# A small expert block put last in a block on one Trainium2 core: its rows reach the sum by a selection, and the stored rows are read back ahead of the next weights

## What is computed

```python
def expert_block(args):
    xb, e = args
    return swiglu(xb, lp['w_eg'][e], lp['w_eu'][e], lp['w_ed'][e])
yb = lax.map(expert_block, (xin, block_e)).reshape(n_rows, d)
return jax.ops.segment_sum(yb[dest] * sw[:, None], st, num_segments=t)
# then: layer_norm(alpha * x + gate * y), rms_norm, x + 0.5 * swiglu(h, w1, w3, w2)
```

## Time and profile before

| what | value |
|---|---|
| three runs, us | 2492.45, 2494.76, 2496.57 (median 2494.76) |
| the profiled execution, us | 2494.52 |
| its span, us | 2493.2 |
| granted PE clock, mean | 0.992 |
| PE busy | 2417.6 us, 97% |
| DVE, ACT, POOL busy | 57%, 42%, 12% |

### The profile page before, as it was taken

The page is one execution under the profiler, slowest core; times in us unless marked ns, Lnnn a source line. Parts: engine busy times, 40 slices in busy tenths (PEclk is TensorE's granted clock), DMA queues, the critical chain, the costliest instruction groups (busy, mean ns, idle before and its releaser), DMA issues.

```text
span 2493.2 us, 30650 instructions
## 1 busy us (share of the span) xinstructions
PE 2417.6 (97%) x12306; PEld 1875.2 (75%) x12306; DVE 1415.3 (57%) x2052; ACT 1040.7 (42%) x1570; POOL 288.8 (12%) x249
## 2 busy tenths in 40 slices
PE   6999999999999989999999899999999999999999
PEld 4877868687777767777666688888888777888887
DVE  3675776768636766555555574344444767543442
ACT  2424434343536346655555462223333555422221
POOL 0010112112132301111111000000122000000000
PEclk9999999999999989999999999999999999999999
DMA  7324243332446378999999822332332111323222
GB/s 277 114 72 168 86 142 126 118 126 75 151 161 224 105 268 348 424 423 424 422 422 423 327 78 91 95 110 86 92 117 77 34 47 64 110 78 108 94 80 80
DMA packets 116227, 428.10 MB, mean 172 GB/s; under 512 B 16040, under 2 KB 30632, under 8 KB 90352
## 3 DMA queue, kind: packets, MB, share of 16 engines
q1 hardware_dynamic: 91488, 377.42, 41.0%
q10 hardware_dynamic: 13440, 25.17, 2.8%
q0 software_dynamic: 11152, 23.49, 2.7%
HBM read 411.60 MB, written 31.72 MB: 178 GB/s over the span
## 4 chain that ended last, share of the span: by engine, by line
PE 75%; DMA 13%; DVE 7%; ACT 4%; issue 1%; SPq 0%; ACTq 0%; POOLq 0%; DVEq 0%
PE bank L754 19%; PE bank L756 18%; PE bank L755 18%; DMA pair<-in_ed 9%; PE bank L1329 2%; DVE HLB L426 1%; PE bank L1310 1%; PE bank L1312 1%; PE bank L1311 1%; PE bank L1367 1%; ACT HLB L415 1%; PE bank L1672 1%; DMA raw<-in_wxbc 1%; DMA raw<-in_wz 1%; PE bank L1695 1%
## 5 line engine op out<-in xcount | busy, mean ns | idle before, releaser
L426 DVE TENSOR_TENSOR HLB<-raw,HLB 128x1024 fp32r<-128x1024 f32 (+1 forms) x286 | 345.6, 1211 | 373.6 <-ACT HLB L415 373.3
L754 PE MATMUL bank<-HTh,HLB 128*128 128x512 f32 (+1 forms) x1358 | 545.2, 401 | 9.9 <-DVE HLB L426 7.5
L756 PE MATMUL bank<-HTh,HLB 128*128 128x512 f32 (+1 forms) x1358 | 528.7, 389 | 0.0
L755 PE MATMUL bank<-HTl,HLB 128*128 128x512 f32 (+1 forms) x1358 | 525.5, 387 | 0.0
L415 ACT ACTIVATE HLB<-raw 128x1024 fp32r<-128x1024 f32 (+1 forms) x294 | 289.5, 991 | 298.6 <-PE bank L756 270.8
L754 PEld LDWEIGHTS bank<-HTh,HLB 128*128 128x128 f32 x1358 | 256.8, 189 | 90.3 <-issue 27.5
L756 PEld LDWEIGHTS bank<-HTh,HLB 128*128 128x128 f32 x1358 | 257.1, 189 | 57.1
L755 PEld LDWEIGHTS bank<-HTl,HLB 128*128 128x128 f32 x1358 | 257.2, 189 | 52.8 <-issue 1.9
L755 PE MATMUL bank<-FAl,HLB 128*128 128x512 f32 x352 | 138.9, 395 | 0.0
L756 PE MATMUL bank<-FAh,HLB 128*128 128x512 f32 x352 | 138.9, 395 | 0.0
L754 PE MATMUL bank<-FAh,HLB 128*128 128x512 f32 x352 | 138.9, 395 | 0.0
(11 more groups left out here) (618 smaller groups left out, 4435.3 us busy)
## 6 DMA issues: line engine op xcount, KB each, us to landing
raw<-in_f SPq DMA_DIRECT2D x120, 512.0 KB, 3.4
ht_pair<-in_eu SPq DMA_DIRECT2D x32, 1024.0 KB, 24.8
pair<-in_ed SPq DMA_DIRECT2D x32, 1024.0 KB, 25.4
raw<-in_wada SPq DMA_DIRECT2D x40, 512.0 KB, 4.0
raw<-in_eg SPq DMA_DIRECT2D x17, 1024.0 KB, 19.8
pair<-in_eu SPq DMA_DIRECT2D x17, 1024.0 KB, 19.6
tmp_pair<-in_eg SPq DMA_DIRECT2D x16, 1024.0 KB, 24.5
ht_pair<-in_eg SPq DMA_DIRECT2D x16, 1024.0 KB, 25.2
```

Source lines behind the costliest of these rows:

```text
L426: self.nc.vector.tensor_tensor(lo, raw, hi.bitcast(F32), ALU.subtract).then_inc(*self.w_lo.next(n))
L754: mm(bank, ah, bh, start=(start and i == 0), stop=False)
L755: mm(bank, ah, bl, start=False, stop=False)
L756: ins = mm(bank, al, bh, start=False, stop=(stop and i == n - 1))
```

## The change

- The order of the blocks becomes 0 to 29, then 31, then 30 (`place_of`), so that a small block is the last, and two whole blocks, 29 and 31, come one behind the other. Positions are still counted 0 to 31.
- On PE and ACT, down of position 30 goes ahead of gate and up of position 31 (the argument `straight`), so no block's work separates it from its own middle. The tiles are loaded in that order, and the last 12 go to places by a new list.
- The kept rows are those of the small block: one eviction and one remainder in place of two each, `YOh` and `YOl` of 128x512, half the columns below partition 64 and half from it on; `tok31` comes from `ixs` by one more instruction. The zeros of `no_rows` cover half rows.
- The four reads of `y_scratch` are issued ahead of the first four tiles of the dense layer, into the parts of `YI` in the order 0, 2, 3, 1 (`back`), each with its own wait.
- The splits of those four tiles move, on ACT from ahead of the combination to behind `act_logs` and between the gains, on DVE from the start of the combination to between its remainders.
- `kept(0, 0)` issues two matmuls without use (`keep_busy`) before it waits for the kept rows.

```diff
-    def __init__(self, nc, small, source, slots, turns, halves, loads, hi_made, lo_made, pe_out):
+    def __init__(self, nc, small, straight, source, slots, turns, halves, loads, hi_made, lo_made, pe_out):
...
-            self.at.append(turns[0][n] if n < len(turns[0]) else turns[1][(n - len(turns[0])) % len(turns[1])])
+            late = n - 6 * len(small) + len(turns[2])
+            self.at.append(turns[0][n] if n < len(turns[0]) else turns[2][late] if late >= 0
+                           else turns[1][(n - len(turns[0])) % len(turns[1])])
...
+        down = [("ed", 0), ("ed", 1)]
         for j in range(n + 1):
+            if j == straight:
+                self.add(j - 1, "down", down)
...
-            if j:
-                self.add(j - 1, "down", [("ed", 0), ("ed", 1)])
+            if j and j != straight:
+                self.add(j - 1, "down", down)
...
-        YOh, YOl = (here("YO" + p, [128, 8, 128], FR) for p in "hl")
+        YOh, YOl = (here("YO" + p, [128, 4, 128], FR) for p in "hl")
...
             for j in range(len(blocks)):
+                if j == S.kept:
+                    down(j - 1)
                 (small_gate_up if tiles.small[j] else gate_up)(j)
...
-                if j:
+                if j and j != S.kept:
                     (small_down if tiles.small[j - 1] else down)(j - 1)
                 turn_mid(j)
-            down(len(blocks) - 1)
+            (small_down if S.kept else down)(len(blocks) - 1)
...
+        def back(i):
+            return YI[:, (0, 2, 3, 1)[i], :, :]
...
                 bank = psum.take(pe, ("yl", t, b))
+                if t == b == 0:
+                    keep_busy(bank, 2)
...
                     k = 2 * b + j
-                    pe.wait_ge(*dve_out.when(("yo", 31, k // 4)))
-                    mm(bank[:, half(j)], YOh[:, k, :], PICK[:, half(t)], start=(j == 0), stop=False)
-                    mm(bank[:, half(j)], YOl[:, k, :], PICK[:, half(t)], start=False, stop=False)
+                    p = slice(64 * (k // 4), 64 * (k // 4) + 64)
+                    pe.wait_ge(*dve_out.when(("yo", 31, 1)))
+                    mm(bank[:, half(j)], YOh[p, k % 4, :], PICK[p, half(t)], start=(j == 0), stop=False)
+                    mm(bank[:, half(j)], YOl[p, k % 4, :], PICK[p, half(t)], start=False, stop=False)
...
+                if j == S.kept:
+                    act.wait_ge(*dve_out.when("wrows"))
+                    activation(YOh[:, :, :], psum[("yo", j, 1)][:, :].rearrange("p (k n) -> p k n", k=4), ACT.Copy,
+                               scale=WROWS[:, KEPT:KEPT + 1]).then_inc(*act_out.next(("yo", j, 1)))
+                    return
...
-                if j == S.kept:
-                    for n in range(2):
-                        activation(YOh[:, 4 * n:4 * n + 4, :], psum[("yo", j, n)][:, :].rearrange("p (k n) -> p k n", k=4),
-                                   ACT.Copy, scale=weight).then_inc(*act_out.next(("yo", j, n)))
-                    return
...
+                if j == S.kept:
+                    last(j - 1)
...
-                if j:
+                if j and j != S.kept:
                     last(j - 1)
...
         def act_combine():
-            ring.hi(act, "f13", 1, itself=True)
             act.wait_ge(*h2_out.when(("rows", 1)))
...
             for b in range(4):
                 square(0, b)
             act_logs()
+            ring.hi(act, "f11", 0, itself=True)
             divisor(0)
             for b in range(4):
                 square(1, b)
                 gains(0, 2 * b)
                 gains(0, 2 * b + 1)
+                if b:
+                    ring.hi(act, *(("f13", 0), ("f11", 1), ("f13", 1))[b - 1], itself=True)
             divisor(1)
...
-                nc.vector.tensor_copy(tok31, ix[:, 0, 31:32]).then_inc(*dve_out.next())
+                nc.vector.tensor_copy(tok31, ixs[:, 0, KEPT:KEPT + 1]).then_inc(*dve_out.next())
                 tiles.free(dve, tiles.last_in[11])
+                dve.wait_ge(*dve_out.now())
+                tensor_scalar(tok31, tok31, K("half", 1), 0.5, ALU.subtract, ALU.mult).then_inc(*dve_out.next())
                 dve.wait_ge(*dve_out.now())
                 for i in range(4):
                     tensor_scalar(PICK[:, cols(i)], K("iota"), 128.0 * i, tok31, ALU.add, ALU.is_equal).then_inc(
                         *dve_out.next("pick"))
-                for n in range(2):
-                    dve.wait_ge(*act_out.when(("yo", j, n)))
-                    dve.wait_ge(*dve_out.when("wrow"))
-                    scalar_tensor_tensor(out=YOl[:, 4 * n:4 * n + 4, :],
-                                         in0=psum[("yo", j, n)][:, :].rearrange("p (k n) -> p k n", k=4),
-                                         scalar=WROW[:, 31:32], in1=YOh[:, 4 * n:4 * n + 4, :].bitcast(F32), op0=ALU.mult,
-                                         op1=ALU.subtract).then_inc(*dve_out.next(("yo", j, n)))
+                dve.wait_ge(*act_out.when(("yo", j, 1)))
+                dve.wait_ge(*dve_out.when("wrows"))
+                scalar_tensor_tensor(out=YOl[:, :, :], in0=psum[("yo", j, 1)][:, :].rearrange("p (k n) -> p k n", k=4),
+                                     scalar=WROWS[:, KEPT:KEPT + 1], in1=YOh[:, :, :].bitcast(F32), op0=ALU.mult,
+                                     op1=ALU.subtract).then_inc(*dve_out.next(("yo", j, 1)))
...
-            ring.lo(dve, "f11", 0, itself=True)
             both(0)
-            ring.lo(dve, "f13", 0, itself=True)
             both(1)
             moe(0, 0)
             moe(0, 1)
-            ring.lo(dve, "f11", 1, itself=True)
             moe(0, 2)
             both(2)
             moe(0, 3)
             both(3)
-            ring.lo(dve, "f13", 1, itself=True)
             moe(1, 0)
             variance(0)
             centre(0, 0, 1)
             moe(1, 1)
             scaled(0, 0, 1)
             centre(0, 2, 3)
+            ring.lo(dve, "f11", 0, itself=True)
             remainder(0, 0)
             moe(1, 2)
             scaled(0, 2, 3)
@@ -3143,10 +3158,15 @@
             remainder(0, 1)
             moe(1, 3)
             scaled(0, 4, 5)
-            remainder(0, 2, 3)
+            remainder(0, 2)
+            ring.lo(dve, "f13", 0, itself=True)
+            remainder(0, 3)
             centre(0, 6, 7)
             scaled(0, 6, 7)
-            remainder(0, 4, 5, 6, 7)
+            remainder(0, 4, 5)
+            ring.lo(dve, "f11", 1, itself=True)
+            remainder(0, 6, 7)
+            ring.lo(dve, "f13", 1, itself=True)
             variance(1)
...
-                nc.gpsimd.memset(YO[1][:, :], 0.0).then_inc(*pool_out.next("zero"))
+                nc.gpsimd.memset(YO[1][:, 0:512], 0.0).then_inc(*pool_out.next("zero"))
                 pool.wait_ge(*pool_out.when("zero"))
+                pool.wait_ge(*dve_out.when("ixs"))
                 nc.gpsimd.indirect_dma_start(
-                    YD, bass.IndirectOffsetOnAxis(ap=ix[:, 1, 31:32], axis=0), YO[1][:, :], None,
-                    bounds_check=1023, oob_is_err=False).then_inc(*S.scattered.next("zero"))
+                    YD_HALVES, bass.IndirectOffsetOnAxis(ap=ixs[:, 1, KEPT:KEPT + 1], axis=0), YO[1][:, 0:512], None,
+                    bounds_check=2047, oob_is_err=False).then_inc(*S.scattered.next("zero"))
...
+        place_of = list(range(30)) + [31, KEPT]
...
-                    found[j] = nc.sync.value_load(eids[0:1, j:j + 1], min_val=0, max_val=31)
+                    found[j] = nc.sync.value_load(eids[0:1, place_of[j]:place_of[j] + 1], min_val=0, max_val=31)
...
-        tiles = ExpertTiles(nc, [j > 1 and j % 2 == 0 for j in range(32)], weights,
+        tiles = ExpertTiles(nc, [b > 1 and b % 2 == 0 for b in place_of], 31, weights,
                             raw_pairs + [p[:, :] for p in pairs + ht_pairs + [tmp_pair, dec_pair]],
-                            ((0, 1, 2, 3, 10, 6, 8, 7, 9, 11), (4, 5, 0, 1, 2, 3, 10, 6, 8, 7, 9, 11)),
+                            ((0, 1, 2, 3, 10, 6, 8, 7, 9, 11), (4, 5, 0, 1, 2, 3, 10, 6, 8, 7, 9, 11),
+                             (0, 1, 2, 3, 10, 4, 5, 11, 6, 8, 7, 9)),
...
-        blocks = [(e, e) for e in range(32)]
+        blocks = [(b, b) for b in place_of]
...
-        for i in (0, 1, 4):
+        sp.wait_ge(*scattered.when(30))
+        sp.wait_ge(*pe_out.when(("xg", 31, 0)))
+        rows = YD.rearrange("(t p k) n -> t p k n", p=128, k=2)
+        for i in range(4):
+            if i == 2:
+                tiles.free(sp, tiles.last_in[4])
+            if i == 3:
+                sp.wait_ge(*pe_out.when(("eu", 31, 3)))
+            nc.sync.dma_start(back(i), rows[i]).then_inc(*y_in[i].next("y"))
+        for i in (0, 1):
             tiles.free(sp, tiles.last_in[i])
         ring.hold()
         ring.load(sp, ring.start_of("f11", 0) + NRAW)
-        sp.wait_ge(*pe_out.when(("eu", 31, 3)))
-        sp.wait_ge(*scattered.when(30))
-        rows = YD.rearrange("(t p k) n -> t p k n", p=128, k=2)
-        for i in range(4):
```

(1 more changed line is left out.)

13 lines of the change are left out of this document (7 added, 6 removed).

## The result

The changed kernel takes 2498.52 us (median of 20 runs, 2496.12 to 2504.12), the kernel before, run beside it, 2496.44 us (20 runs). The ratio is 1.0014, 95% interval 1.0008 to 1.0020: **slower, by 2 to 5 us**, where 4 us faster was forecast and 2495.2 was the upper end of the range.

What follows compares the result with a forecast made beforehand. PE, busy 97% of the span, was taken as the bound, with DMA, then DVE, limiting it near the end. From the 2494.76 us median, -6.5 + 2.5 = -4.0 gave 2490.7 us; 8-in-10 range 2487.2 to 2495.2.

Steps and rivals of the forecast that it cites:

- Part 1: New order of the last blocks, up to the selection: nothing won, 0.3 us lost, selection at 1419.1 against 1418.80.
- walk to the small down: PE's work from 1378.67 us, reordered: a 2.15 us wait, block 31's down 5.7, small down 3.6, ending at 1417.3.
- the kept rows take the same one eviction and one remainder as before, 1.8: Between small down and selection: PE waits 1.8 us for the kept rows, from 1417.3 to 1419.1.
- fill that wait: The two keep_busy matmuls fit into PE's wait for the kept rows; overrunning it would cost some tenths.
- Part 2: Reads ahead of the first tiles: just hidden, 4.9 us plus 1.6 of clock, 6.5 together by the end of squares(0).
- Part 3: Four splits moved behind 1439.3 us, where DVE is the bound: 2.5 us lost, ends 1.0 and 3.6.
- idle time: DVE's gaps from 1440 us to PE's wait at 1453.51: about 0.7 us of the moved splits fits in.
- Rival 3: PE's clock stays at 1.2 GHz through 96 narrow products from 1455.5 on: 8.6 us lost, 2499.3 us; chance 0.04.
- Rival 2: Late hand-over of pieces between whole blocks, or reads added only at 1423.6: costs 1.5 to 3, 2493.0 us; chance 0.16.
- Rival 4: Reads not really ahead, since block 31's scatter waits for block 29's: 2495.7 us; chance 0.03.

Runs made afterwards that it cites:

- b1: Kernel before without the overflow part and its branch: 2493.75 us against 2495.45 for the kernel before, ratio 0.9992 [0.9982, 1.0002].
- b3: Kernel before with only the four splits moved to the change's places: 2499.08 us against 2494.63 for the kernel before, ratio 1.0017.
- h2: Changed kernel with only the fourth read and the first tiles held until PE ends the last down: 2495.31 us (one run).
- e3: Changed kernel with third and fourth read and first four tiles held until PE ends the last down: 2495.88 us (one run).
- e6: Changed kernel with its four reads issued behind the first tiles again: 2499.29 us against 2495.45 for the kernel before, ratio 1.0016.
- e4: Changed kernel, splits out of the busy stretch: two behind DVE's second addition, two behind the first half's last remainder: 2495.91 us, ratio 0.9995 to the kernel before.
- c0: Changed kernel, two splits in DVE's and ACT's idle times, two behind the first half's last remainder: 2496.18 us, ratio 1.0004 to the kernel before.
- e2: Changed kernel without the overflow part and its branch: 2495.53 us against 2496.62 for the kernel before, ratio 0.9994.
- c2: Changed kernel with c0's places of the splits and without the overflow part and its branch: 2492.90 us, ratio 0.9995 to the kernel before.
- e7: Changed kernel with e3's held reads and tiles and e4's places of the splits together: 2501.06 us, ratio 1.0017 to the kernel before.
- e9: e7 plus two keep_busy products ahead of block 31's down: 2501.46 us against 2495.45 for the kernel before, ratio 1.0021.
- c1: Changed kernel with c0's places of the splits and e3's held reads and tiles: 2493.73 us, ratio 0.9996 to the kernel before.
- c3: c1 plus two keep_busy products in the wait ahead of block 31's down: 2494.62 us against 2495.75 for the kernel before, ratio 0.9995.

## Why the prediction was wrong

In time the forecast was 4.0 us under the kernel before, and the change came out 2.1 us (medians) to 3.5 us (ratio) above it. In length, of one profile each, forecast and kernel differ by 8.6 us: 92.7 - 4.0 = 88.7 against 97.3. By its own steps:

- **Part 1, walk to the small down: right but for the clock.** The wait of 2.15 us is 2.14; gate-up and middle of the small block, put at 9.0 us, took 8.9 (1410.26 to 1419.17); the small down, 3.6, took 3.65. Block 31's down was put at 5.7 and took 7.40, 1.7 late. That is not the new order's own: b1 and b3 have the old order and 7.40 both. The profile of before was a lucky one here (that down was slow in 11 of the 14 profiles without `keep_busy` ahead of it), and one profile doesn't tell that.
- **Part 1, "the kept rows take the same one eviction and one remainder as before, 1.8": this is the step that failed.** The rows were ready at 1424.35, 1.5 us behind the down. But I read PE's 1.66 us wait as all that stood there, and under it lay the arrival of the code behind the branch, done 0.5 us earlier. With the third read in the way the code comes 2 us later (h2 against e3), and the cover doesn't grow. From the end of the small down to the selection it took 5.67 us: 3.06 of hole, 2.60 of `keep_busy`, which "fill that wait" no longer, since they too are behind the branch. 3.9 us late.
- **Part 2: the reads are hidden, as said, but not by being ahead.** e6 has them behind the tiles and the same time. The 6.5 us that they were to win by the end of `squares(0)` are 0.3 (1439.27 against 1443.32 - 4.34), because the selection is 5 us late and it and `keep_busy` run at the low clock behind the hole: from its start to that end 14.8 us instead of 13.7, 1.1 late.
- **Part 3: right mechanism, size too small.** Put at 2.5 with ends 1.0 and 3.6; 5.0 in the change, 3.5 alone (b3), 4.2 given back with the splits out of the stretch (e4). DVE is at 5.00 of 5 us over three windows: the four splits, 4.8 us of DVE's work, are paid nearly in full. How much of it the lower clock adds isn't separated. Moving two into idle time and two behind the last remainder gives 3.4 of it back (c0), which the 0.7 us of "idle time" in the text would not have allowed: the gaps that c0 uses for the first two lie ahead of and around the end of `squares(0)`, outside the stretch that I counted.
- **Rivals.** Rival 3, the slower side, had the right engine state at the wrong place: the clock didn't stay down in the products from 1455.5 on, it fell behind PE's holes, in `squares(1)` (3.5 us for 1.9) and behind the branch. Rival 2's price was for late splits and late reads; neither was late. Rival 4 is out. None had the branch, and with a chance of 0.04 on slower I was sure of what one profile can't show.

Terms: 1.7 + 3.9 + 1.1 + (5.0 - 2.5) = 9.2 of the 8.6 us, within 0.6.

The Trainium skill, Runtime: NRT & Kernel Launch, "Instruction fetch mechanics", has the rule that I didn't weigh: a taken branch out of the prefetched window makes the engine fetch its target page by DMA before it goes on. By that a hole must stand behind this branch wherever nothing else covers it. The trace agrees: none with the branch gone (e2, c2), 0.74 to 1.00 us with the third read held (e3, e7, e9, c1, c3), 2.88 to 3.31 with it in the queue.

## What to carry to other kernels

A branch that is jumped over isn't free: look for the instruction packet behind it in the DMA rows and for the wait that covers it, and before you shorten that wait or put transfers ahead of it, ask what else was under it. A transfer started earlier takes its DMA time from something, and that may be the code. Where two engines are at 100% of several windows, price a moved instruction in full, and before adding two remedies check that neither holds back what the other needs.
